# A transformer block on one core: the shared expert ahead of the gate in the weight stream, the router's tables in another order, the row requests third

## The reference, cut

```python
x = layer_norm(ALPHA * x + g1 * mix) * ln1_g + ln1_b
h = layer_norm(x) * (1.0 + sc2) + sh2
ffn = moe_ffn(h, ...)
x = layer_norm(ALPHA * x + g2 * ffn) * ln2_g + ln2_b      # g2: columns of silu(c) @ w_ada

def moe_ffn(h, ...):
    scores = sigmoid(hf @ router_w)                       # 256 x 64
    biased = scores + router_bias
    grp_score = top_k(biased.reshape(T, 8, 8), 2)[0].sum(-1)
    # the 4 best of 8 groups stay, of their experts the 8 best of biased are taken
    gate = scores of these 8, divided by their sum, times 2.5
    # every token's row goes to its 8 experts:
    # (silu(xb @ w_gate[e]) * (xb @ w_up[e])) @ w_down[e], weighed and summed
    shared = (silu(hf @ sh_gate) * (hf @ sh_up)) @ sh_down
    return routed + shared
```

## Time and profile before

| | us |
|---|---|
| median of 3 runs | 1905.09 |
| their range | 1904.33 to 1908.37 |
| the profiled execution | 1909.98 |
| its span, first to last instruction | 1908.2 |
| TensorE busy in the span | 1757.9 |
| mean granted TensorE clock | 0.968 of full speed |

### The profile page before, as it was taken

How to read it: one execution, slowest core, us unless ns; L and a number is a source line. 1 busy time by engine, 2 the same in 40 slices (tenths; PEclk the granted TensorE clock), 3 DMA queues, 4 the chain that set the end, 5 groups by cost and what they waited for, 6 DMA issues and landing times.

```text
span 1908.2 us, 29833 instructions
## 1 busy us (share of the span) xinstructions
PE 1757.9 (92%) x12438; PEld 1270.5 (67%) x12438; DVE 925.8 (49%) x1344; ACT 670.5 (35%) x950; POOL 500.5 (26%) x362
## 2 busy tenths in 40 slices
PE   5999999999769999999999969899997979979998
PEld 2899997786534444444444457678886749968887
DVE  4276924676721211212122268564457875766453
ACT  2445347442301211111111245454334343335342
POOL 1387877100133444444454200000000001400000
PEclk9999999999879999999999979999998989989999
DMA  8555551166599998979979644155444500024442
GB/s 360 184 189 177 179 187 55 67 239 255 230 423 424 419 381 329 371 277 394 389 259 420 249 152 155 46 213 197 178 177 163 188 22 26 4 89 167 178 176 96
DMA packets 64970, 414.40 MB, mean 217 GB/s; under 512 B 20613, under 2 KB 20629, under 8 KB 24529
## 3 DMA queue, kind: packets, MB, share of 16 engines
q0 software_dynamic: 37808, 218.05, 28.5%
q1 hardware_dynamic: 26624, 192.95, 27.4%
q10 hardware_dynamic: 416, 1.66, 0.2%
HBM read 550.99 MB, written 2.10 MB: 290 GB/s over the span
## 4 chain that ended last, share of the span: by engine, by line
PE 79%; DVE 8%; DMA 7%; issue 2%; ACT 2%; another core or an unknown queue 1%; POOL 1%; DVEq 0%; POOLq 0%; ACTq 0%
PE ps L1070 12%; PE ps L804 10%; PE ps L806 10%; PE ps L805 10%; PE ps L1089 6%; PE ps L842 5%; PE ps L844 5%; PE ps L843 5%; PE ps L860 3%; PE ps L1103 3%; PE ps L1448 3%; PE ps L1056 1%; DMA ring<-in_moe_dn,arena 1%; DMA arena<-in_moe_dn,arena 1%; DMA ring<-in_weights 1%
## 5 line engine op out<-in xcount | busy, mean ns | idle before, releaser
L805 PE MATMUL ps<-ring_lo,arena_r 128*128 128x512 f32 x888 | 349.7, 394 | 0.0
L1070 PE MATMUL ps<-arena 128*32 128x512 f32 (+2 forms) x832 | 245.8, 603 | 13.8 <-ACT arena L1750 7.2
L844 PE MATMUL ps<-arena_r,ring_lo 128*128 128x256 f32 x768 | 217.3, 283 | 0.0
L804 PE MATMUL ps<-arena_r 128*128 128x512 f32 x528 | 210.2, 398 | 2.2 <-DVE arena_r L2263 2.2
L1070 PE MATMUL ps<-ring,arena 128*32 128x512 f32 (+2 forms) x560 | 203.1, 604 | 5.3 <-issue 2.2
L806 PE MATMUL ps<-arena_r 128*128 128x512 f32 x528 | 206.6, 391 | 0.0
L805 PEld LDWEIGHTS ps<-ring_lo,arena_r 128*128 128x128 f32 x888 | 169.6, 191 | 33.9
L2237 DVE TENSOR_TENSOR ring_lo<-ring,arena_r 128x2048 fp32r<-128x2048 f32 x66 | 150.7, 2291 | 76.2 <-ACT arena_r L1635 76.1
L1635 ACT ACTIVATE high<-ring 128x2048 fp32r<-128x2048 f32 x62 | 118.5, 1915 | 123.2 <-PE ps L842 71.7
L2614 DVE SCALAR_TENSOR_TENSOR arena<-ps,arena 128x256 f32<-128x256 f32 x38 | 18.4, 484 | 278.9 <-ACT arena L1766 278.9
L842 PE MATMUL ps<-arena_r,high 128*128 128x256 f32 x528 | 150.9, 286 | 2.4 <-DVE ring_lo L2237 1.3
(11 more groups left out here) (468 smaller groups left out, 3605.2 us busy)
## 6 DMA issues: line engine op xcount, KB each, us to landing
ring<-in_weights SPq DMA_DIRECT2D x183, 1024.0 KB, 4.8
arena<-in_ln POOLq DMA_DIRECT2D x2, 1024.0 KB, 7.7
arena<-in_lora POOLq DMA_DIRECT2D x1, 1152.0 KB, 5.4
arena<-in_x POOLq DMA_DIRECT2D x1, 1024.0 KB, 12.4
h_rows<-arena ACTq DMA_DIRECT2D x1, 1024.0 KB, 11.9
arena<-in_bands POOLq DMA_DIRECT2D x1, 1024.0 KB, 11.5
arena<-in_rw_kk_ka POOLq DMA_DIRECT2D x2, 512.0 KB, 7.4
arena<-in_rw_w0a POOLq DMA_DIRECT2D x1, 1024.0 KB, 4.9
```

The costliest lines, as they stand in the source:

```text
L804: head = pe.matmul(dst, hi, w, start=start, stop=False, skip_group_check=True)
L805: pe.matmul(dst, hi, rest, start=False, stop=False, skip_group_check=True)
L844: mm = pe.matmul(dst, rest, hi[:, k, :], start=False, stop=(k == count - 1))
L1070: mm = pe.matmul(pb("moe", mu("gu", i))[at, :], x_cols[:, k, at], gu_w[s % SETS][:, k * 512:(k + 1) * 512], start=(k == 0), stop=(k == KC ...
```

## The change

- The three `moe` tiles come ahead of the four `gate2` tiles in the stream: `moe` is 80 to 82 (slots 2, 3, 4), `gate2` is 83 to 86 (slots 5, 0, 1, 2). The PSUM stage `gate2` is behind `router`.
- TensorE's `partial("gate2", 0)` and `(…, 1)` and the two `spread_sum` move from around h2's transposes and the router to behind `count_tokens`, between the small sums. The shared expert's gate and up products come in four quarters, `shared_half`: one between the router's product and its sums, three behind the sums. The row table's sums come in two halves, between the two passes of the shared down product.
- ScalarE rounds the shared expert's first two tiles ahead of `modulated` and of the store of h2, the third ahead of the router's sigmoid; it copies the gate sums behind the first `gated`. These sums lie in another buffer (half of buffer 3), so ScalarE waits for `h2_stored`.
- VectorE forms the rests of all three tiles ahead of the choice; the 16 `MAX8` for the groups are ten element-wise maxima and minima, a tree; both `weighed` stand ahead of `placed`; the token's one-hot is made in two halves, behind the pair's.
- POOL requests units 0 and 1, then the first two gathers, and then units 2 and 3, ahead of which it waits for all six ring slots. The ring holds units 2 and 3 (before: 0 and 3).

```diff
-               ("w_o", 4), ("ada2", 8), ("gate2", 4), ("moe", 3), ("hy_in", 10), ("hy_out", 4),
+               ("w_o", 4), ("ada2", 8), ("moe", 3), ("gate2", 4), ("hy_in", 10), ("hy_out", 4),
...
-               ("ada2", 8), ("gate2", 4), ("h2T", 4), ("router", 3), ("moe", 0), ("a0T", 4), ("f", 3), ("hy_in", 10), ("qkT", 4),
+               ("ada2", 8), ("h2T", 4), ("router", 3), ("gate2", 4), ("moe", 0), ("a0T", 4), ("f", 3), ("hy_in", 10), ("qkT", 4),
...
+        gate2_parts = buf(3)[:, D:2 * D].rearrange("p (s n) -> p s n", s=2)
...
-        ring_sets = {0: 3, 3: 0}
+        ring_sets = {2: 0, 3: 3}
...
-        gu_w = [ring_set(0), buf(9, 2), buf(7, 2), ring_set(3), buf(5, 2), spare.rearrange("p s n -> p (s n)")]
-        dn_w = [ring[:, 5, :], buf(11), buf(12), ring[:, 2, :], buf(13), twin[:, 0:TW]]
+        gu_w = [buf(9, 2), buf(7, 2), ring_set(2), ring_set(3), buf(5, 2), spare.rearrange("p s n -> p (s n)")]
+        dn_w = [buf(11), buf(12), ring[:, 2, :], ring[:, 5, :], buf(13), twin[:, 0:TW]]
...
-            for s in (3, 4, 5):
-                pool.wait_ge(sem(f"w_used{s}"), (TILES["hy_in"] - 1 - s) // SLOTS + 1)
+            pool.wait_ge(sem("x1_ready"), 1)
             gate_up(0)
             down(0)
-            pool.wait_ge(sem("x1_ready"), 1)
             gate_up(1)
             down(1)
-            gate_up(2)
-            down(2)
-            pool.wait_ge(sem("down_done1"), 1)
-            gate_up(3)
-            down(3)
             pool.wait_ge(sem("h2_stored"), 16)
             pool.wait_ge(sem("tables"), 3)
             gather(0)
             gather(1)
+            pool.wait_ge(sem("down_done1"), 1)
+            for s in range(SLOTS):
+                pool.wait_ge(sem(f"w_used{s}"), (TILES["hy_in"] - 1 - s) // SLOTS + 1)
+            gate_up(2)
+            down(2)
+            gate_up(3)
+            down(3)
             gate_up(5)
...
-                units = UNITS[TURNED.get(stage, "moe")]
-                for b in range(BANKS):
-                    moe = len(MOE) // MOE_BANKS if stage != "moe" and b >= BANKS - MOE_BANKS else 0
-                    pe.wait_ge(sem(f"ps_read{b}"), units_in_bank(units, b) + moe)
+                def banks_read():
+                    units = UNITS[TURNED.get(stage, "moe")]
+                    for b in range(BANKS):
+                        moe = len(MOE) // MOE_BANKS if stage != "moe" and b >= BANKS - MOE_BANKS else 0
+                        pe.wait_ge(sem(f"ps_read{b}"), units_in_bank(units, b) + moe)
+
+                if stage != "moe":
+                    banks_read()
                 if stage == "moe":
-                    gate_up(0, 0, 0, 0, False)
                     pe.wait_ge(sem("marks"), 1)
                     count_tokens()
-                    gate_up(0, 0, 0, 1, False, beside=rank_experts)
+                    partial("gate2", 0)
+                    for t in range(NT):
+                        pe.wait_ge(sem(f"hid{t}"), 1)
+                    pe.wait_ge(sem("marks"), 2)
+                    rank_experts()
+                    partial("gate2", 1)
+                    pe.wait_ge(sem("marks"), 3)
+                    sum_extra()
+                    spread_sum("gate2", 0)
+                    pe.wait_ge(sem("marks"), 4)
+                    sum_bases()
+                    spread_sum("gate2", 1)
+                    banks_read()
                     turn_hidden(0, 0, False)
                     turn_hidden(0, 1, False)
                     down(0, 2, 0, 0, True, True)
+                    row_table()
...
+            def shared_half(t, half):
+
+                if t == 0:
+                    split("moe", half)
+                for k in range(4 * half, 4 * half + 4):
+                    head, mm = three(ps[:, 5 - t, :], (hT_hi[:, k, tokens(t)], hT_lo[:, k, tokens(t)]), "moe", half,
+                                     slice((k % 4) * 512, (k % 4 + 1) * 512), k == 0, k == KC - 1)
+                    if k == 4 * half:
+                        carry(head)
+                if half:
+                    mm.then_inc(sem(f"gu_full{t}"), 1)
+                if t == NT - 1:
+                    if half:
+                        used_late("moe", half)
+                    else:
+                        used(mm, "moe", half)
...
+            def rank_experts():
+
+                pe.matmul(rank_sums, ones[0:EXPERTS, :], ranked, start=True, stop=True,
+                          skip_group_check=True).then_inc(sem("slots"), 1)
...
+            def slot_table(dst, mark, qs):
+                for q in qs:
+                    mm = pe.matmul(dst, token_mark[:, q, :], mark[:, q, :], start=(q == 0), stop=(q == 15),
+                                   skip_group_check=True)
+                    if q == 0:
+                        carry(mm)
+                return mm
...
+            def row_table():
+
+                for half in range(2):
+                    pe.wait_ge(sem("marks"), 5 + half)
+                    mm = slot_table(row_sums, row_mark, range(8 * half, 8 * half + 8))
+                mm.then_inc(sem("slots"), 1)
...
-                slot_table(row_sums, row_mark).then_inc(sem("slots"), 1)
-                pe.wait_ge(sem("marks"), 6)
-                slot_table(gate_sums, gate_mark.rearrange("p q v n -> p q (v n)")).then_inc(sem("slots"), 1)
+                pe.wait_ge(sem("marks"), 7)
+                slot_table(gate_sums, gate_mark.rearrange("p q v n -> p q (v n)"), range(16)).then_inc(sem("slots"), 1)
                 turn_rows(0)
...
-            partial("gate2", 0)
             modulated(pe, "ada2", 0)
             turn_half("h2T", 0)
             modulated(pe, "ada2", 1)
             turn_half("h2T", 1)
-            partial("gate2", 1)
             all_read(pe, "h2T", 4)
             pe.wait_ge(sem("params1_in"), 80)
             stack("router", router_w, EXPERTS, (hT_hi, hT_lo))
-            spread_sum("gate2", 0)
-            spread_sum("gate2", 1)
+            shared_half(0, 0)
             stack_sums("router", const("sum2", EXPERTS), EXPERTS)
+            shared_half(1, 0)
+            shared_half(0, 1)
+            shared_half(1, 1)
             experts("moe")
             routed()
...
+                    partial_sums("gate2", 0, 1)
+                    for u in range(2):
+                        full(act, "gate2", 2 * u + 1)
+                        step.read(fn(mod_gate[:, u * 512:(u + 1) * 512], pb("gate2", 2 * u + 1), ACT.Copy), "gate2", 2 * u + 1)
...
+            round_tiles("moe", 0, 1)
             modulated(act, "ada2", 1)
             act.dma_start(h2_rows.rearrange("(t p) n -> p t n", p=P), h_tok).then_inc(sem("h2_stored"), 16)
             hT_parts("h2T")
-            partial_sums("gate2", 0, 1)
-            round_tiles("moe", 0, 1)
+            round_tile("moe", 2)
+            warm(ACT.Sigmoid)
             stacked_sums("router")
-            warm(ACT.Sigmoid)
-            for u in range(2):
-                full(act, "gate2", 2 * u + 1)
-                step.read(fn(mod_gate[:, u * 512:(u + 1) * 512], pb("gate2", 2 * u + 1), ACT.Copy), "gate2", 2 * u + 1)
             for t in range(NT):
                 full(act, "router", 1 + t)
                 step.read(fn(rt_scores[:, t, :], pb("router", 1 + t)[:, 0:EXPERTS], ACT.Sigmoid), "router", 1 + t)
-            round_tile("moe", 2)
+            warm(ACT.Silu)
+            act.wait_ge(sem("h2_stored"), 16)
             experts("moe")
...
+                between()
                 for t in range(NT):
                     step(dve.max(key[:, t, :], unit[:, t, :]))
-                between()
...
-                    weighed(0, 0)
-                    placed(lambda: weighed(0, 1))
                     for t in range(NT):
-                        hidden(0, t)
+                        weighed(0, t)
+                    placed(lambda: hidden(0, 0))
+                    hidden(0, 1)
...
-            rest_of_tiles("moe", 0, 1)
+            rest_of_tiles("moe", 0, 1, 2)
...
-            for q in range(2 * EGROUPS):
-                step(dve.max(best[:, q, :], flat(biased)[:, q * 8:(q + 1) * 8]))
-            step(tt(group_sums, best[:, :, 0], best[:, :, 1], A))
+            by_two = flat(biased).rearrange("p (q i e) -> p q i e", q=2 * EGROUPS, e=2)
+            step(tt(most4, by_two[:, :, :, 0], by_two[:, :, :, 1], ALU.max))
+            step(tt(next4, by_two[:, :, :, 0], by_two[:, :, :, 1], ALU.min))
+            for most, next_, new_most, new_next, low in ((most4, next4, most2, next2, low2), (most2, next2, most1, next1, low1)):
+                step(tt(low, most[:, :, 0::2], most[:, :, 1::2], ALU.min))
+                step(tt(new_next, next_[:, :, 0::2], next_[:, :, 1::2], ALU.max))
+                step(tt(new_most, most[:, :, 0::2], most[:, :, 1::2], ALU.max))
+                step(tt(new_next, new_next, low, ALU.max))
+            step(tt(group_sums.unsqueeze(2), most1, next1, A))
...
-            rest_of_tile("moe", 2)
...
```

(6 more changed lines are left out.)

53 lines of the change are left out of this document (20 added, 33 removed).

## The result

The changed kernel takes 1912.97 us in the median of 15 runs (1901.51 to 1918.27), the kernel before 1905.68 us in 15 runs. The two medians are 7.3 us apart, but the runs scatter over 17 us and 12 us, and the ratio over all of them is 1.0028, with a 95% interval of 1.0014 to 1.0041: slower by 5.3 us, between 2.7 and 7.8. The text goes by this ratio.

What follows compares the result with a forecast made beforehand. The saturated weight queue was taken as the bound: a stream 3.3 us later plus 0.1 us for clock recovery brought the profiled 1909.98 to 1913.4 us, so 1908.4 on the median's footing, range 1902 to 1913.

Steps and rivals of the forecast that it cites:

- step 2: Ahead of `placed`: shared quarters, router sums and token count take 13.6 us; VectorE's marks 2.7 us early, tree gains nothing.
- The form of the sum: Weight queue: request start-up cancels, so the stream is later by delta = T − 527.65, +3.3 us.
- T: POOL's request of units 2 and 3, once all six ring slots are free: forecast at 530.9.
- Step 1: Router's product on TensorE: begins at half clock, 1.9 us lost, end at 490.1 instead of 488.2.
- S: Start of `placed` on VectorE: forecast at 503.7, against 505.86 before.
- E: `expert_rows` on VectorE, 8.8 us behind S: forecast at 512.5.
- Steps 3 to 5: From S to T: E 512.5, row list 526.4, gathers requested 527.3, gate marks 529.75, T 530.9.
- What is hidden: Routed stage: rows turned 11.9 us earlier, nothing kept; weight wait grows from 4.0 to about 19 us; clock recovery 0.1 us.
- A: First gather: the rows were the bound, so TensorE keeps the 11.9 us: 1893.2; chance 0.11.
- B: Slot 4's release behind the gate marks: T later, deciding from 531.5 on, 1910.1 or 1911.3; chance 0.22 with D.
- C: Router's product: the clock stays up, S is 1.9 us earlier, 1906.5; chance 0.12.
- D: ScalarE's rounding of tile 81 is late, pushing `modulated`, h2 and router by 1 to 2 us: 1910; chance 0.22 with B.

Runs made afterwards that it cites:

- rows_fifth: Changed kernel, but units 2 and 3 are requested ahead of the gathers, without waiting for slot 4's release: 1.0022 of the kernel before (+4.2 us).
- after_warm: Changed kernel with four added products of constants on TensorE around h2's transposes, read by nobody: 1.0011 of the kernel before (+2.1 us).
- tree_alone: Kernel before with only the 16 MAX8 replaced by ten maxima and minima: one run, no ratio; first request 1.0 us sooner in one profile.
- before_rows_fourth: Kernel before with the first two gathers requested ahead of unit 3 instead of behind it: 1.0009 of the kernel before (+1.7 us).
- third_warm: Changed kernel with unit 2 requested directly behind unit 1, and the four added products of after_warm: 0.9978 of the kernel before (−4.2 us).

## Why the prediction was right

1908.4 us with a range of 1902 to 1913 was forecast on the footing of 1905.09, that is +3.3; measured were +5.3 (2.7 to 7.8), on that footing 1910.4 us. The measured median of 1912.97 us lies in the range by 0.03 us, and that is luck. So is the side on which it came out: same and slower had 0.44 and 0.43, and slower came. What held is the mechanism, and in the profile its size to 0.8 us (+3.3 forecast, +4.1 in distance). Two sums of the prediction are 0.1 us off by rounding (13.6 for 13.5 in step 2, 1908.4 for 1908.5).

- **The form of the sum.** Right. The hole in the DMA share lies at 525 to 533. Delta from the measured T is 531.28 − 527.65 = +3.6; the wait ended 4.3 later. In distance it is +3.4 by the sum and +4.1 measured. Where the missing 0.6 us lies is not shown. The 12 us behind 533 went at 392 GB/s, against 423 before the hole, which would be 0.8 us. But the queue of rows_fifth also ran dry and started again, and there the wait ended 0.2 us sooner than its sum. What differs is that in the changed kernel the two gathers ran alone between two restarts (86 GB/s from 528 to 530); that the start-up cancels, as the prediction has it, holds in one of the two kernels.
- **Step 1, the clock.** Right in kind, as after_warm shows. The size was short: the prediction took 3.7 us at half clock, and so 1.9 us lost. No row gives the 3.7; it lies between what the two stretches of the earlier trace rows suggest. Measured are 2.55 us lost (6.22 − 3.67). The product ended at 491.06, not 490.1, since its first stretch was all at 0.50 and the next at 0.69. Two other terms were too long and gave it back: the router's sums held up the quarters for 0.36 us (493.85 to 494.21), not 1.1, so that S was 504.08 for 503.7, and from S to E it was 8.4 us, not 8.8. The rule of the Trainium skill, "TensorE: Matmul & The Clock Gate", section "Part 1: The HAM clock gate (the "warmup" mystery)", is that an idle array falls to 1.2 GHz. The trace agrees: the first 3.6 us of the product were granted 0.50.
- **Step 2, VectorE.** The marks were early by 1.3 us (501.2 against `count_tokens` at 502.50), not 2.7, but early. The 2.7 were counted to S, and the marks are needed 1.5 us ahead of it. That the tree gains nothing there fits the changed kernel by this slack, since the tree saves 1.0; it would not hold for the kernel before, as tree_alone shows.
- **Steps 3 to 5.** E 512.52 (512.5 forecast), row list 526.62 (526.4), gathers 527.46 (527.3), gate marks 529.94 (529.75), T 531.28 (530.9). POOL's wait before unit 2 ended with a product of L1083, the gate sums, as said.
- **What is hidden.** TensorE turned its rows at 532.55, 12.8 us sooner, and kept nothing. But the prediction looked for it all in the waits: 15 to 20 us for `in_moe_gu` before 675, about 19 in the working. There were 11.3 us, and 15.2 with the rows (3.9 + 2.7 + 5.9 + 2.7). From the first turned rows to the end of the last long wait it is now 142.5 us instead of 125.5, of which TensorE is busy for 125.8 instead of 120.5, at a granted clock of 0.92 instead of 0.98. So 5.3 of the 17.1 us went into the same products at a lower clock, for which the prediction had 0.1 us; they cost nothing here, since the queue set the end. And "never waits for weights again" behind 670.8 holds only for long waits: there are five of 0.4 to 1.0 us in the kernel before.
- **The rivals.** A fell by the result and by before_rows_fourth. B, slower because T is later than 531.5, is close to what happened, though T stayed under its border (531.28) and the 0.6 us from elsewhere did the rest. C fell: the clock did go down, and in the four profiles of this order without added products the router's product took 5.99 to 6.38 us, never 3.67. D did not show: the store of h2 went out at 480.46 against 480.24.

## What to carry to other kernels

Where one queue is full without a break up to a wait for its data, count that wait's end from the queue's first request and its bytes; a hole of the consumer before it is free, and the time that the queue stands dry is lost (here by 0.6 us more than by the bytes alone in one kernel, 0.2 less in another). When transfers are reordered, ask of every slot what is the last thing that holds it: here half of the ring was free 20 us before the request that waited for all of it. And when filler work is moved out of a gap on TensorE, look at what runs behind the gap, since it may now begin at half clock.

## What the runs showed of the hardware

Short gaps of TensorE can lower its clock without one long gap among them: with gaps of 1.9, 1.4 and 2.4 us around two groups of transposes (3.35 busy us in 8.8) it was granted 0.73 there and 0.50 in the 3.6 us behind. With four products of constants between them the gaps were 1.02, 0.56 and 1.54 us, and it was granted 1.00 there and behind, in after_warm and in third_warm. And the length of the saturated stream, 160.3 to 160.5 us in seven profiles, repeated better than anything else measured here; by the profile it moves 66 to 67 MB at 414 to 416 GB/s.
